# Gathered experts: two tiles in the second projection, one in the joint attention

## What is computed

```python
z = a @ lw['w_in']                                   # 1024 -> 9240 columns
y_m = mlstm_chunkwise(...)                           # from z
y_f = fox_block(...)                                 # causal softmax with forgetting, 16 heads, from z
h = h + merge @ lw['w_out']
# experts: 8 heads x top 16 of 16384 for each token
act = gelu(einsum('thkd,td->thk', u_tab[idx], xb))
out = einsum('thk,thkd->td', g * act, v_tab[idx])
h = h + out
```

## Time and profile before

| | us |
|---|---|
| three runs | 5664.17, 5664.45, 5665.58 (median 5664.45) |
| profiled execution | 5658.33 |
| its span | 5656.7 |
| second projection, in the span | 1756 to 2402 |
| gates | 2402 to 2429 |
| joint attention | 2429 to 3365 |
| its 80 steps, from maximum to maximum | 2443 to 3350 |

### The profile page before, as it was taken

The page is one execution under the profiler, slowest core; times in us unless marked ns, Lnnn a source line. Parts: engine busy times, 40 slices in busy tenths (PEclk is TensorE's granted clock), DMA queues, the critical chain, the costliest instruction groups (busy, mean ns, idle before and its releaser), DMA issues. The chain is left out here.

```text
span 5656.7 us, 51607 instructions
## 1 busy us (share of the span) xinstructions
PE 4689.4 (83%) x16510; PEld 2846.4 (50%) x16510; DVE 3078.0 (54%) x6244; ACT 1030.8 (18%) x1850; POOL 1219.0 (22%) x1162
## 2 busy tenths in 40 slices
PE   4999678667984999957777758884699999999989
PEld 3555453343662555545555545564555545544544
DVE  1000231121476544468888861758877777777752
ACT  2000230001110111134444431111200000000013
POOL 0000002200002333223333320000044444444410
PEclk9999788767997999966666659997999999999999
DMA  3333323327755988778888868773599999999961
GB/s 100 108 114 105 99 83 128 108 86 270 276 197 197 356 306 311 284 272 322 331 323 320 317 243 326 275 255 119 190 381 419 418 412 419 411 419 418 414 263 58
DMA packets 464521, 1478.13 MB, mean 261 GB/s; under 512 B 38290, under 2 KB 204994, under 8 KB 361442
## 3 DMA queue, kind: packets, MB, share of 16 engines
q0 software_dynamic: 119872, 824.76, 36.5%
q1 hardware_dynamic: 344482, 651.36, 32.1%
HBM read 1370.06 MB, written 115.38 MB: 263 GB/s over the span
## 5 line engine op out<-in xcount | busy, mean ns | idle before, releaser
L1922 POOL DMA_INDIRECT ex_uv<-in_uv,ex_here x768 | 1049.2, 1366 | 1918.6 <-DVE ex_acc L1992 1783.6
L1979 DVE CUSTOM_DVE_ANT_0 ex_uv<-ex_uv,ex_xp 128x1024 f32<-128x1024 f32 x768 | 912.5, 1218 | 289.3 <-DMA ex_uv<-in_uv,ex_here 238.5
L1992 DVE SCALAR_TENSOR_TENSOR ex_acc<-ex_uv,ex_wt,ex_acc 128x1024 f32<-128x1024 f32 x768 | 941.8, 1282 | 9.5 <-DVE ex_wt L1983 1.1
L2261 PE MATMUL exp_psum_dn<-exp_dn_big,exp_dn_gg 128*128 128x512 f32 x1536 | 688.0, 598 | 28.4 <-DVE exp_dn_gg L2183 28.4
L2252 PE MATMUL exp_psum_dn<-exp_dn_xT,exp_dn_big 128*128 128x384 f32 x2048 | 683.5, 487 | 14.5 <-DMA exp_dn_big<-in_ud 14.5
L259 PE MATMUL proj_psum_acc<-proj_w,aT_later 128*128 128x385 f32 x1920 | 625.9, 488 | 74.2 <-DMA proj_w<-in_w_in 67.4
L2252 PEld LDWEIGHTS exp_psum_dn<-exp_dn_xT,exp_dn_big 128*128 128x128 f32 x2048 | 390.1, 191 | 314.2 <-issue 61.9
L259 PEld LDWEIGHTS proj_psum_acc<-proj_w,aT_later 128*128 128x128 f32 x1920 | 364.9, 190 | 334.8 <-issue 70.4
L259 PE MATMUL proj_psum_acc<-proj_w,aT 128*128 128x385 f32 x1536 | 499.7, 487 | 8.9 <-DMA proj_w<-in_w_in 8.9
L2261 PEld LDWEIGHTS exp_psum_dn<-exp_dn_big,exp_dn_gg 128*128 128x128 f32 x1536 | 292.4, 192 | 379.8 <-issue 352.3
L685 PE MATMUL att_psum_fy<-att_fv,att_fprobT 128*128 128x64 f32 x1152 | 238.4, 363 | 240.7 <-ACT att_fprobT L732 240.6
(11 more groups left out here) (368 smaller groups left out, 4864.2 us busy)
## 6 DMA issues: line engine op xcount, KB each, us to landing
proj_w<-in_w_in SPq DMA_DIRECT2D x48, 1540.0 KB, 7.1
rt_w<-in_w_q SPq DMA_DIRECT2D x36, 2048.0 KB, 8.3
exp_dn_big<-in_ud SPq DMA_DIRECT2D x128, 512.0 KB, 11.2
exp_dn_big<-in_vd SPq DMA_DIRECT2D x128, 512.0 KB, 8.0
scratch_z<-proj_zs SPq DMA_DIRECT2D x216, 192.5 KB, 2.7
rt_w<-in_w_br_m SPq DMA_DIRECT2D x18, 2048.0 KB, 10.8
rt_w<-in_w_br_f SPq DMA_DIRECT2D x18, 2048.0 KB, 10.9
rt_w<-in_w_out SPq DMA_DIRECT2D x18, 2048.0 KB, 8.2
```

The lines of the kernel that those rows point to most:

```text
L1922: pool.indirect_dma_start(self.uv[:, slot * self.G + j, :], None, self.uv_tab, bass.IndirectOffsetOnAxis(ap=self.here[:, at, j:j + 1], axi ...
L1979: dve.tensor_tensor_reduce(self.uv[:, slot, 0:D], self.uv[:, slot, 0:D], self.xp[:], 1.0, 0.0, ALU.mult, ALU.add, self.dot[:, p % 2, j:j + ...
L1992: dve.scalar_tensor_tensor(out=self.acc[:, j % 2, :], in0=self.uv[:, slot, D:2 * D], scalar=self.wt[:, p % 2, j:j + 1], in1=self.acc[:, j ...
L2261: mm = pe.matmul(self.banks[t][:, n * 512:(n + 1) * 512], self.gg[:, 4 + q % 4, t * P:(t + 1) * P], self.big[:, 4 + q % 4, n * 512:(n + 1) ...
```

## The change

`stage_project` gets a number of tiles and cuts its loop of 8 iterations into as many spans, here two of four. In a span one tile of experts is done, so that an iteration holds eight groups in place of four. Their acts stand ahead of copies 0, 1, 3, 5, 7, 9, 11 and 13. Between the spans SP stores the first tile's sum, waits until x and h have been taken, and loads the next. `dve_all` opens and ends each tile. The joint attention gets one tile in place of two, so `share` puts half as many units in a half step. All computations stay.

```diff
-def stage_project(nc, aT, w_in, z, t0, nt, ex=None):
+def stage_project(nc, aT, w_in, z, t0, nt, ex=None, tiles=1):
...
+        spans = [(t, t * NI // tiles, (t + 1) * NI // tiles) for t in range(tiles)]
         if ex:
-            ex.begin(st, NI)
+            ex.begin(st, NI // tiles, tiles)
+            groups = {p * PER // ex.GPI: p for p in range(ex.GPI)}
...
+            for t, i0, i1 in spans:
+                if t >= 1:
+                    ex.store(sp, t - 1)
+                    sp.wait_ge(ex.xp_set, t)
+                    sp.wait_ge(ex.acc_set, t)
+                    ex.load(sp, t)
+                with sp.Fori(i0, min(i1, NI - 1)) as i:
...
-            with act.Fori(0, NI) as i:
-                for j in range(PER):
-                    if ex and j % (PER // ex.GPI) == 0 and j // (PER // ex.GPI) < ex.GPI:
-                        ex.act_group(act, i, j // (PER // ex.GPI))
...
+            for t, i0, i1 in spans:
+                if ex:
+                    ex.act_tile(act, t)
+                with act.Fori(i0, i1) as i:
+                    for j in range(PER):
+                        if ex and j in groups:
+                            ex.act_group(act, i, groups[j])
...
-        self.dve_tile(dve, 0)
-        with dve.Fori(0, self.NI) as i:
-            for p in range(self.GPI):
-                self.dve_units(dve, i, p, (0, 2 * self.G + 1))
-        self.dve_end(dve, 0)
+        for t in range(self.nt):
+            self.dve_tile(dve, t)
+            with dve.Fori(t * self.NI, (t + 1) * self.NI) as i:
+                for p in range(self.GPI):
+                    self.dve_units(dve, i, p, (0, 2 * self.G + 1))
+            self.dve_end(dve, t)
...
-                stage_project(nc, aT_later, A["w_in"], z, FIRST, NT - FIRST, ex)
+                stage_project(nc, aT_later, A["w_in"], z, FIRST, NT - FIRST, ex, 2)
...
-                stage_attend(nc, K, z, gates, C, m, T, FIRST - 1, PT, ex, 2)
+                stage_attend(nc, K, z, gates, C, m, T, FIRST - 1, PT, ex, 1)
```

More of the change, by code:

```diff
@@ L233, in store @@
                              zs[:, j % SLOTS, :]).then_inc(out[j % SLOTS], 16)
-            with sp.Fori(0, NI - 1) as i:
-                for u in range(U):
-                    for j in range(u * nt, (u + 1) * nt):
-                        store(i, j)
-                    sp.dma_start(w[:, u], w_in_v[:, :, bass.ds(i * (U * CW) + (U + u) * CW, CW)]
-                                 ).then_inc(w_in_u[u], 16)
+            for t, i0, i1 in spans:
[5 more added lines that the diff above has]
+                with sp.Fori(i0, min(i1, NI - 1)) as i:
+                    for u in range(U):
+                        for j in range(u * nt, (u + 1) * nt):
+                            store(i, j)
+                        sp.dma_start(w[:, u], w_in_v[:, :, bass.ds(i * (U * CW) + (U + u) * CW, CW)]
+                                     ).then_inc(w_in_u[u], 16)
             for j in range(PER):
@@ L246, in _ @@
             if ex:
-                ex.store(sp, 0)
+                ex.store(sp, tiles - 1)
                 ex.stored_all(sp)
@@ L265, in _ @@
             act.sem_inc(read, SLOTS)
[L266 to L274 removed]
+            for t, i0, i1 in spans:
[5 more added lines that the diff above has]
+                            ex.act_group(act, i, groups[j])
+                        act.wait_ge(summed, i * PER + j + 1)
+                        act.wait_ge(out[j % SLOTS], (i * (PER // SLOTS) + j // SLOTS) * 16)
+                        act.copy(zs[:, j % SLOTS, :], acc[j % SLOTS][:, 0:CW]).then_inc(read, 1)
         if ex:
```

5 lines of the change are left out of this document (removed).

## The result

The changed kernel takes 5726.73 us (median of 5 runs, 5704.52 to 5737.83) against 5664.45 us before (5662.77 to 5668.18): a ratio of 1.0104 with the interval 1.0081 to 1.0127. It is slower by 62 us. The profiled execution took 5726.7 us, its span is 5725.1 us and its mean granted clock 0.882.

What follows compares the result with a forecast made beforehand. The projection was taken as bound by PE, then by DMA with the second tile; the attention by a ring through PE, DVE and ACT. +234 and -172 us gave +62, 5726 us from 5664.45, range 5615 to 5825.

Steps and rivals of the forecast that it cites:

- The term for the projection: Second projection: with a second tile of experts DMA binds, 880 us in place of 646, +234 us.
- the one for the attention: Joint attention: with one tile of experts fewer, 80 steps save 2.15 us each, -172 us.
- the ring of the attention: Joint attention: each step goes through PE, DVE and ACT in turn, with expert units between; 11.3 us a step.
- 842 us by engine time: Projection: DMA time with both tiles, from the stage's own gather, weight and store times at a share of 1.03.
- The holes of 12 us: Projection: 12 us added to the DMA time for holes.
- The change of tile: Projection, between the two tiles: 6 us added, since eight gathers in flight cover 21 us; uncovered 30 us.
- The idle part: Attention: PE's idle time in a step falls from 2.9 to 1.9 us with half the expert units.
- the interpolation: Attention: PE's clock read as 0.78, between 0.65 here and 0.91 in the first attention; PE needs 7.2 us a step.
- rival (a): Attention: PE's clock comes to 0.91, saving 255 us; with +210 in the projection the kernel takes 5619 us; chance 0.19.
- (b): Projection: DMA does not bind, DVE's 720 us do, +74; sum -98 us, kernel 5566 us; chance 0.04.
- (c): Projection: slow z stores through SP's queue delay ACT and make DMA holes, +320; kernel +148, 5812 us; chance 0.14.
- (d): Projection: engines move only 383 GB/s at a full share, +269; kernel +97, 5761 us; chance 0.06.

Runs made afterwards that it cites:

- the further products: Four more 128x128 products, read by nobody, ahead of each attention mix in the changed kernel: 5619.3 us against 5726.7 without; attention 662.7 against 761.2.

## Why the prediction was right, and where it was not

The sum came out as forecast: 5726 us predicted and 5726.73 measured, +62 us by the medians and +68 by the profiled executions, where +62 was forecast. That it came so close is luck. The term for the projection was 25 us too high, the one for the attention 26 us too favourable, and the two errors cancelled. The direction isn't luck: a stage bound by DMA lost more than the ring of the attention gained, as described.

**What bounds each stage.** Right on both. The projection has turned from PE to DMA (share 0.99; half the bytes give 153 us back, half the dot 6 us). The attention has lost DVE as its near bound (62%, predicted 63%), and goes by the ring, with PE at a mean clock of 0.70.

**The projection, +234 predicted, +209 measured.** The failing step is the rate. I took 842 us by engine time, since the stage carried its own mix, and set the 416 GB/s of the dense stage as the lower end, because of its larger pieces. That reason was weak: most of what the dense stage moves are the same gathers of 8 KB rows, as its DMA shows for the kernel before (4200 to 5300 us):

```profile
q0 software_dynamic: 45461, 328.94, 72.3%
q1 hardware_dynamic: 31668, 128.94, 28.8%
```

The steady stretch of the projection moved 414 GB/s. With that rate the stage's 341 MB (399 GB/s over 856 us) are 825 us, and the start, change and end of 13, 15 and 8 us make 861, against 859 measured. The holes of 12 us which I had added don't exist: from the start to the change (1802 to 2186 us), and from there to the end (2234 to 2570 us), the share is 1.02. The terms explain 21 of the 25 us (880 predicted for the stage); the other 4 are the base, which I had set at 646 us and which is 650 as dated here. The change of tile cost 15 us in place of the 6 I gave it. I counted the hole as DVE's stop, 20 to 30 us, and it is POOL's, 35 us, since no gather is issued until the first add has freed a buffer. If the gathers in flight cover 21 us of it, as I had estimated, 14 us are left. Loading x early gave 12 to 13 us back.

**PE's slack.** I wrote that PE would no longer set the end and that a lower clock costs it slack only. Right: it is busy 663 of 856 us at 0.90, which is 77% and not 71%, as its clock fell, and it stands 146 us behind ACT.

**The attention, -172 predicted, -146 measured.** The idle part was right: (761 - 609)/80 = 1.9 us a step, as predicted from the five steps of the timeline. The clock was not: 0.70 in place of 0.78, so PE is busy 7.6 us a step and not 7.2, which makes 32 us over 80 steps by these rounded figures and accounts for the whole miss of 26 us. The step that failed is the interpolation between this stage's own 0.65 and the 0.91 of the first attention. The right end of that line was another ring; this one has 0.76 without any experts. At much the same busy share of PE (80% and 83%) the clock of this stage is 0.70 and 0.76, while in the first attention 81% stood beside 0.91: one stage's clock could not be read from another's. The conversion between clock and step held for the whole step: I had put a step at a clock of 0.91 at 8.1 us and the saving at 255 us; when the further products brought the clock to 0.92, the step was 8.3 us and the saving 244 us. Its parts did not hold: PE's own work was 5.6 us a step (448/80) and not 6.3, and 2.7 us were waits or further products, where 1.9 idle were predicted. The kernel then took 5619.3 us, for which rival (a) had 5619; that these meet so closely is luck too, since its terms were 210 and 255 us against 208 and 244. So rival (a) names a true mechanism, which this code alone does not set off.

**The rivals.** (b) is excluded by the DMA share, and by half the bytes: only then the projection comes to 706 us, near the 720 that it takes from DVE. (c) began and cost nothing: weights land after 42 us and ACT waits 169 us for stores of z, with 22 us as the longest wait. Its threshold was not reached: a store of z lands after 24.7 us where the trace has it (the kernel with the early load), and the rival wanted more than 36. ACT is late even so, but that makes no hole in DMA; the share is 1.02 throughout the steady part. So the threshold asked the wrong thing, or at least not enough: what counts is whether ACT is so late that DVE stops and gathers are no longer issued. DVE waits 57 us for the act in place of 261 before. No run made stores slower to test it. (d) is excluded by 414 GB/s. The HBM limit of 358 GB/s that the Trainium skill (DMA: Bandwidth & Descriptors, Specifications) gives does not bind here: by the prediction's estimate it would have made the projection 976 us, but 414 GB/s were sustained over 350 us.

**What the prediction did not see** is that a whole tile was the wrong size of step. It wrote that 110 us of DMA are free in the projection and that the tile uses them up, and had thereby the two slopes in hand, but not the consequence: twelve groups more would have gone for 4.5 us, and the attention gives most for the first of them.

ACT's wait for the dots and the wait for fprobT (135 us, predicted near 120) came as described.

## What to carry to other kernels

When work is moved from a stage that is bound by one thing to a stage with another resource free, work out how much of the free resource there is and move that much: here 17% of DMA time took 12 groups for 4.5 us, and each one beyond cost about 10 us. Look at both slopes, since the stage that is relieved gives less and less once its own bound is gone. Where TensorE waits for others and its granted clock is low, and no other engine is near full, a few products of no use ahead of its waiting point are a cheap test; they gave 98 us in the form of the stage where VectorE was 62% busy, some 10 us of the kernel where it was 80%, and nothing where it was 85%.

## What the runs showed of the hardware that I had not expected

- A stage whose gathers, weight loads and stores run together held 414 GB/s at a share of 1.02 for 350 us, nearly the dense stage's 416, where gathers are 329 of 458 MB and the rest are large loads.
- With the engines full of gathers, a load of weights on the other queue went from 11.4 to 42.0 us until landing, at the same bytes.
- Half the bytes in each gather did not take half the time of the engines. 136.6 MB took 58.9% of 690 us, 406 us; 275.1 MB took 78.4% of 846 us, 663 us. That is 61% of the time, at nearly the same number of packets (37,516 and 37,786).
- The spread of the changed kernel, 33 us over five runs against 5 us for the kernel before (10 and 12 us in its two later rounds), goes with the mean clock of the whole execution: 0.886 for the run of 5704.5 us, 0.884 for 5720.1, 0.882 for 5726.7, 0.880 for 5730.7 and 0.879 for 5737.8. Why the attention has another clock from one run to the next with the same work isn't settled.
